# A chunked delta rule in two transformer blocks: the triangular inverses start from solved diagonal blocks of 16 instead of from the identity

## What is computed

```python
kk = heads(k * k_k)
kk = kk / jnp.maximum(jnp.sqrt(jnp.sum(kk * kk, -1, keepdims=True)), 1e-12)
k = k * (1 + (a - 1) * k_a)
decay = jnp.exp(-jnp.exp(heads(w)))
def step(S, inp):
    r_t, w_t, k_t, v_t, kk_t, b_t = inp
    sa = jnp.einsum('bhvk,bhk->bhv', S, -kk_t)
    S = S * w_t[:, :, None, :] + sa[..., None] * b_t[:, :, None, :] + v_t[..., None] * k_t[:, :, None, :]
    return S, jnp.einsum('bhvk,bhk->bhv', S, r_t)
S0 = jnp.zeros((B, H, N, N), f32)
_, y = lax.scan(step, S0, tuple(to_time(t) for t in (rh, decay, kh, vh, kk, kk * ah)))
...
bonus = jnp.sum(rh * kh * r_k, -1, keepdims=True) * vh
```

## Time and profile before

| | |
|---|---|
| median of 3 runs | 1495.6 us (1494.48 to 1495.86) |
| profiled execution | 1490.96 us |
| its span | 1489.2 us |
| mean granted clock of TensorE | 0.977 |
| DVE busy | 883.4 us, 59% |
| ACT busy | 630.5 us, 42% |
| POOL busy | 73.8 us, 5% |
| chain that ended last | PE 72%, DVE 21%, ACT 5% |
| longest group of DVE | weight remainders L1592, 374.7 us |

### The profile page before, as it was taken

The page is one execution under the profiler, slowest core; times in us unless marked ns, Lnnn a source line. Parts: engine busy times, 40 slices in busy tenths (PEclk is TensorE's granted clock), DMA queues, the critical chain, the costliest instruction groups (busy, mean ns, idle before and its releaser), DMA issues.

```text
span 1489.2 us, 21642 instructions
## 1 busy us (share of the span) xinstructions
PE 1401.2 (94%) x9280; PEld 1254.6 (84%) x9280; DVE 883.4 (59%) x1293; ACT 630.5 (42%) x899; POOL 73.8 (5%) x42
## 2 busy tenths in 40 slices
PE   7999899999899999999899999899988989799998
PEld 4676898998899997876699999898988888599997
DVE  5167534537654447554655445798988755565554
ACT  1343342534444344444543443543445544554443
POOL 0011030000200002100200000100000000000000
PEclk9999999999999999999999999998999999899999
DMA  9423000005655564622175555644544434155650
GB/s 288 147 77 113 1 1 2 1 1 198 208 188 181 189 196 129 211 85 86 57 254 172 196 172 168 198 129 161 161 133 135 148 114 163 63 198 170 196 187 29
DMA packets 154383, 204.96 MB, mean 138 GB/s; under 512 B 7440, under 2 KB 128400, under 8 KB 154160
## 3 DMA queue, kind: packets, MB, share of 16 engines
q1 hardware_dynamic: 154288, 203.59, 41.7%
HBM read 202.53 MB, written 1.05 MB: 137 GB/s over the span
## 4 chain that ended last, share of the span: by engine, by line
PE 72%; DVE 21%; ACT 5%; issue 1%; DMA 0%; SPq 0%; DVEq 0%; ACTq 0%
PE PS L465 18%; PE PS L466 17%; PE PS L467 17%; DVE PH L2049 6%; DVE WW L1592 4%; PE PS L762 3%; PE PS L749 3%; PE PS L766 2%; PE PS L665 2%; DVE AL L1631 2%; PE PS L610 1%; PE PS L715 1%; DVE PA L1855 1%; PE PS L630 1%; PE PS L646 1%
## 5 line engine op out<-in xcount | busy, mean ns | idle before, releaser
L1592 DVE TENSOR_TENSOR WW<-RG,WW 128x2048 fp32r<-128x2048 f32 x164 | 374.7, 2290 | 213.4 <-ACT WW L1118 213.2
L465 PE MATMUL PS<-AH,WW 128*128 128x256 f32 x1664 | 480.4, 289 | 16.6 <-DVE AL L1631 12.8
L466 PE MATMUL PS<-AL,WW 128*128 128x256 f32 x1664 | 475.3, 286 | 0.0
L467 PE MATMUL PS<-AH,WW 128*128 128x256 f32 x1664 | 475.1, 286 | 0.0
L1118 ACT ACTIVATE WW<-RG 128x2048 fp32r<-128x2048 f32 x164 | 311.4, 1906 | 90.7 <-PE PS L467 88.2
L465 PEld LDWEIGHTS PS<-AH,WW 128*128 128x128 f32 x1664 | 323.9, 195 | 23.7 <-issue 12.3
L466 PEld LDWEIGHTS PS<-AL,WW 128*128 128x128 f32 x1664 | 324.0, 195 | 1.6 <-issue 0.2
L467 PEld LDWEIGHTS PS<-AH,WW 128*128 128x128 f32 x1664 | 323.7, 195 | 0.0
L465 PE MATMUL PS<-WW,HH 128*128 128x512 f32 x304 | 118.8, 391 | 0.1
L466 PE MATMUL PS<-WW,HH 128*128 128x512 f32 x304 | 118.7, 390 | 0.0
L467 PE MATMUL PS<-WW,HL 128*128 128x512 f32 x304 | 118.3, 389 | 0.0
(11 more groups left out here) (270 smaller groups left out, 1771.9 us busy)
## 6 DMA issues: line engine op xcount, KB each, us to landing
RG<-in_ffn_w_in SPq DMA_DIRECT2D x44, 1024.0 KB, 5.1
RG<-in_w_ff SPq DMA_DIRECT2D x32, 1024.0 KB, 5.4
RG<-in_w_in SPq DMA_DIRECT2D x30, 1024.0 KB, 5.2
RG<-in_ffn_w_down SPq DMA_DIRECT2D x22, 1024.0 KB, 4.9
RG<-in_w_rkv SPq DMA_DIRECT2D x12, 1024.0 KB, 5.3
RG<-in_moba_w_qkv SPq DMA_DIRECT2D x12, 1024.0 KB, 5.2
RG<-in_w_o SPq DMA_DIRECT2D x4, 1024.0 KB, 9.2
RG<-in_wx_kv SPq DMA_DIRECT2D x4, 1024.0 KB, 5.9
```

The lines of the kernel that those rows point to most:

```text
L465: e.matmul(o, lh, rh, start=start, stop=False)
L466: e.matmul(o, lh, rl, start=False, stop=False)
L467: return e.matmul(o, ll, rh, start=False, stop=stop)
L1592: v.tensor_tensor(WL[lo_n % NW], ring(SPLIT[lo_n]), WH[lo_n % NW].bitcast(F32), ALU.subtract).then_inc(s_lo, 1)
```

## The change

1. **Norms on eight columns.** The sums of squares go to 8 columns (4 products against two columns). DVE bounds them with 1e-24, POOL raises them to the power -0.5, ACT spreads them to 512 columns in `qq`, and PE turns that back into the layout of the keys (`norm_spread`). Square root and reciprocal of 512 columns leave. The bonus is also taken on 8 columns and spread by the read.
2. **Two sets of buffers** for decays, k, r and kk. k always uses bank 0 and r bank 1. The key chain of step j-1 runs on DVE after the decay work of step j. All forms of half 0 are made after the key stage.
3. **Blocks of 16.** Levels 0 to 3 leave in both halves. In their place: the diagonal blocks are formed again in products of 64 by 128 by 128 (`block_form`), masked and gathered on DVE to 16 by 16 values per matrix (`block`), each row is spread by a product with a selector matrix of 0 and 1 (`block_rows`, a new ring piece `sel` of 128 by 1920 made on the host), ACT copies the rows, and DVE solves row after row (`block_inverse`), widens the result to 128 by 128 (`block_wide`), and PE turns it (`block_turn`). W uses two banks instead of four.
4. **Order.** Half 1's blocks are formed and solved inside half 0's inverse. POOL's gain and gate work is in 12 operations of 512 columns and starts after the first state. The memory turn is spread over two levels, and the group norm steps and `wo0` have new places.
5. **First pieces in two banks** (`chan_two`): the two column halves of the first piece run together over each quarter of the activation, at four places (gated FFN twice, last FFN, convolution).

Constants and norms (the first lines are SP's list):

```diff
 EARLY = ['lora', 'g1', 'v00', 'v01', 'v10', 'v11', 'k0', 'r0', 'k1', 'r1', 'k2', 'r2', 'k3', 'r3',
-         'g2', 'gn']
+         'g2', 'gn', 'sel']
...
+    put('m16', ((f >> 4) == (p >> 4)) & (p < f))
+    put('blk', (f >> 4) == (p >> 4))
+    put('eye16', (p % 16) == np.arange(16)[None, :])
...
+    return np.concatenate([((k // 16) == (m // 16)) & (k % 16 == r) for r in range(15)], 1).astype(np.float32)
...
+            piece('sel', (lambda r: r[:, 0:1920], a['sel']))
...
+            def norm_sums(j):
...
+                for q in range(4):
+                    t = e.matmul(PS[6][:, 2 * q:2 * q + 2], qq[:, q * 128:q * 128 + 128], cst('sel2'), start=True, stop=True)
+                t.then_inc(s_nm, 1)
+
+            def norm_spread(j):
+                e.wait_ge(s_nq, j + 1)
+                for q in range(4):
+                    t = e.matmul(PS[6][:, q * 128:q * 128 + 128], qq[:, q * 128:q * 128 + 128], ident, start=True, stop=True)
+                t.then_inc(s_nb, 1)
...
+                        t = e.matmul(PS[7][:, 4 * tt + 2 * m:4 * tt + 2 * m + 2],
+                                     rS2[j % 2][:, m * 256 + tt * 128:m * 256 + tt * 128 + 128], cst('sel2'), start=True, stop=True)
...
+                g.wait_ge(s_nx, j + 1)
+                own_pool.done()
+                g.tensor_tensor(RN, RN, POW, ALU.pow).then_inc(s_nr, 1)
```

PE: first pieces, blocks, the key stage and what follows it:

```diff
+            def chan_two(name, b0, b1, ready):
...
+                for k in range(8):
+                    if k % 2 == 0:
+                        e.wait_ge(s_tl, ready + k // 2 + 1)
+                    for m, b in enumerate((b0, b1)):
+                        t = mm3(e, PS[b][:, m * 256:(m + 1) * 256], wsl(name, 256, k, m * 128, m * 128 + 128), act_k(k), k == 0, k == 7)
+                t.then_inc(s_wdone, 1)
...
+            def block_form(half, pair):
+
...
+                    for t in range(2):
+                        c, h, m, pp = prob(half, pair + 2 * t, n)
+                        o_ = 256 * t + 128 * (n // 2)
+                        x = e.matmul(PS[2 + n % 2][:, o_:o_ + 128], BE[pp, m, c * 128:c * 128 + 128], AR[pp, m, c, 0, :],
+                                     start=True, stop=True)
+                    if n >= 2:
+                        x.then_inc(s_ef, 1)
...
+            def block_rows(half, b):
...
+                for r in ROWS[b]:
+                    _, lo, hi = row_at(r)
+                    t = e.matmul(PS[2 + b % 2][:, lo:hi].rearrange("p (i q) -> p i q", i=16), ring('sel')[:, 128 * r:128 * r + 128],
+                                 DB[half][:, :, r:16], start=True, stop=True)
+                t.then_inc(s_se, 1)
...
+            def block_turn(half, g, b):
...
+                for n in range(4):
+                    ns = slice(n * 128, n * 128 + 128)
+                    t = e.transpose(PS[b][:, ns], Zi[:, g, ns], ident)
+                t.then_inc(s_zt, 1)
...
+                    if j:
+                        e.wait_ge(*((s_kq, j), (s_rs_, j))[n])
                     for m in range(2):
+                        if m and n:
+                            norm_sums(j)
+                            if j == 3:
+                                block_rows(0, 2)
+                                block_rows(0, 3)
+                        elif m and j:
+                            norm_spread(j - 1)
...
+                    if n == 0 and j < 3:
+                        decay(j + 1)
+                    elif n == 0:
+                        block_rows(0, 0)
+                        block_rows(0, 1)
                 if j:
                     bonus(j - 1)
+                if j in (1, 2):
+                    block_form(0, j - 1)
+                if j == 3:
+                    block_rows(0, 4)
...
+            e.wait_ge(s_dt, 4)
+            gates(0)
...
+            e.wait_ge(s_sn, 5)
+            e.wait_ge(s_gta, 2)
+            for g in range(4):
+                block_turn(0, g, 2 + g)
+            e.wait_ge(s_gta, 4)
+            e.wait_ge(s_gk, 2)
+            e.wait_ge(s_xb, 2)
+            for g in range(4):
+                form(0, g, [0, 1, 2, 3])
...
+            e.wait_ge(s_xb, 4)
+            turned(0, [4, 5])
```

The halves on PE:

```diff
-                for l in range(7):
+                for l in range(4, 7):
                     for g in range(4):
...
+                    if half:
+                        if l < 6:
+                            memory_turn((2 * l - 8, 2 * l - 7))
+                    elif l < 6:
+                        block_form(1, l - 4)
+                    else:
+                        block_rows(1, 0)
+                        block_rows(1, 1)
+                    for g in range(4):
+                        invert_xz(half, l, g)
+                if half == 0:
+                    block_rows(1, 2)
+                    block_rows(1, 3)
+                e.wait_ge(s_wt, 12 * half + 12)
                 rhs_of(half, 0)
                 rhs_of(half, 1)
-                e.wait_ge(s_xz, 24 * half + 24)
+                if half == 0:
+                    block_rows(1, 4)
```

ACT in the halves, DVE in the key stage and the solve:

```diff
+            def rows_out(half, b):
+                n = sum(16 * (16 - r) for r in ROWS[b])
+                s.wait_ge(s_se, 5 * half + b + 1)
+                s.activation(NS[half][b], PS[2 + b % 2][:, 0:n], ACT.Copy, bias=0.0, scale=1.0).then_inc(s_sn, 1)
...
+                    for g in range(4):
+                        inverted(half, l, g)
+                    if half and l < 6:
+                        memory_turned((2 * l - 8, 2 * l - 7))
...
+                    if (half, l) == (1, 5):
+                        ahead('wo0', 0)
...
-                    if half == 1 and l == 4:
-                        ahead('wo0', 0)
...
+
...
+                v.wait_ge(s_dx, 4 * half + o + 1)
+                own_dve(v.tensor_reduce(db[:, 4 * o:4 * o + 4, :], td.rearrange("p (n b q) -> p n q b", n=4, b=8), AX, ALU.add))
...
+                    own_dve(v.tensor_copy(XC[half], eye16))
...
+            def block_inverse(half):
...
+                    for r in ROWS[b]:
+                        _, lo, hi = row_at(r)
+                        p3 = v3(PR[half][:, 0:hi - lo], 16 - r)
+                        own_dve.done()
+                        own_dve(v.tensor_tensor(p3, v3(NS[half][b][:, lo:hi], 16 - r), xc[:, :, r:16], ALU.mult))
+                        own_dve.done()
+                        own_dve(v.tensor_reduce(xc[:, :, r], p3, AX, ALU.add))
+
+            def block_wide(half, g):
...
+                for e_ in range(2):
+                    o = 8 * (g % 2) + 4 * e_ + 2 * (g // 2)
+                    z = Zi[:, g, :].rearrange("p (u e b r) -> p u e b r", u=2, e=2, b=8)[:, :, e_, :, :]
+                    xc = XC[half][:, o:o + 2, :].unsqueeze(2).broadcast_to([128, 2, 8, 16])
+                    t = v.tensor_tensor(z, xc, blk[:, 0:2, :].rearrange("p n (b r) -> p n b r", b=8), ALU.mult)
+                t.then_inc(s_zb, 1)
...
+            for j in range(4):
+                carried(j)
+                if j >= 2:
+                    block(0, 2 * j - 4)
+                    block(0, 2 * j - 3)
+                if j:
+                    keys(j - 1)
+                if j >= 2:
+                    bonus(j - 2)
+                if j < 3:
+                    decay(j + 1)
+                v.wait_ge(s_nm, j + 1)
+                own_dve.done()
+                v.tensor_scalar(RN, PS[6][:, 0:8], 1e-24, None, ALU.max).then_inc(s_nx, 1)
+            block_inverse(0)
             for g in range(4):
+                block_wide(0, g)
+            bonus(2)
+            keys(3)
+            for g in range(4):
+                formed(0, g, [0, 1, 2, 3])
                 unit(0, g)
             bonus(3)
```

The halves on DVE, and POOL:

```diff
-                for l in range(7):
...
+                    elif half == 0:
+                        block_inverse(1)
+                    elif l == 4:
+                        for step in (0, 1, 3):
+                            group_norm(1, 0, 0, step)
+                    elif l == 5:
+                        for step in (5, 6, 7):
+                            group_norm(1, 0, 0, step)
                         ahead('wo0', 0)
+                        for step in (0, 1):
+                            group_norm(2, 1, 0, step)
+                    else:
+                        for step in (3, 5, 6, 7):
+                            group_norm(2, 1, 0, step)
...
                 if half == 0:
+                    for g in range(4):
+                        block_wide(1, g)
...
-            g.wait_ge(s_xz, 8)
+            g.wait_ge(s_ss, 1)
...
+            for tt in range(2):
+                for h in range(2):
+                    sl = slice(h * 512, h * 512 + 512)
+                    own_pool(g.tensor_tensor(BV[:, tt, sl], BV[:, tt, sl], gn[:, 1024 + h * 512:1536 + h * 512], ALU.add))
+                    own_pool.done()
+                    own_pool(g.tensor_tensor(BV[:, tt, sl], BV[:, tt, sl], GT_[:, tt, sl], ALU.mult))
+                    own_pool.done()
```

(2 more changed lines are left out.)

368 lines of the change are left out of this document (219 added, 149 removed).

## The result

The changed kernel takes 1447.4 us (median of four runs, 1444.44 to 1451.19) against 1495.73 before: ratio 0.9685, 95% interval 0.9669 to 0.9702, 48 us faster. The forecast was 1443, its range 1428 to 1456. The profiled execution has a span of 1442.6 us against 1489.2, 46.6 less.

What follows compares the result with a forecast made beforehand. PE, busy 94% of the span, was taken as the bound; 34.8 - 13.3 + 24.9 + 6.0 = 52.4 us gained, giving 1438.6 in the profiled execution and 1443 at the median, range 1428 to 1456.

Steps and rivals of the forecast that it cites:

- Half 0 up to its last product: Key stage and matrix inverse of half 0: last product at 189.2 us against 224.0, 34.8 gained.
- PE sets the pace, 18.3 a step: Key stage, half 0: PE work of 18.3 us per step against 12.5 on DVE, up to step 3's norm sums.
- 1.5 for 864 columns of row products: Key stage, step 3: row products on PE priced by columns, 0.22 us per 128, 1.5 us.
- The 1.0 us for the clock: Half 0, PE going from idle to paced work at 142 to 156: 1.0 us added, between 0 and 1.9.
- The row chain: Half 0's row solve on DVE: 30 dependent small operations, 10.2 us, plus one POOL meeting of 1.2.
- small matmuls cost their weight load: Rival, key stage: small matmuls cost 0.19 us each, 5 us, first-piece gain mostly taken by remainders; 1450 us, chance 0.12.
- Rest of half 0: After half 0's last product to outputs' end: 39.4 us against 26.1, 13.3 lost, with DVE widenings priced beside POOL.
- no turn-taking on the port: Rival, half 1's widenings beside POOL: they run through at 2.7 us or in pairs; 1432 us, chance 0.20.
- Half 1: Half 1's last forms and inverse: 47.8 us against 72.7, 24.9 gained, with a hole of nearly 8 us.
- First pieces: Two-bank first pieces: 3.0 and 2.7 us at gated FFNs, 0.3 conv, 0 last FFN; 6.0 gained, between 1 and 8.
- low clock in more places: Rival: low clock over all of level 4 and after both holes, about 10 us more; 1453 us, chance 0.14.
- the power on POOL: Key stage norms on 8 columns: hidden under about 4 us; rival slower than before, over 17 us each, chance 0.03.

Runs made afterwards that it cites:

- e12: The control: the changed kernel itself, unedited, measured again beside the kernel before; 1448.9 us, ratio 0.9695.
- e11: Changed kernel with the four norm-sum products made four times in each of the four key-stage steps; 1468.2 us, ratio 0.9811.
- e1: Changed kernel with POOL's twelve gain and gate operations started after half 0's level-4 X and Z copies, not after the state; 1439.5 us, ratio 0.9644.
- e2: Changed kernel with POOL's twelve gain and gate operations waiting for the last widening of half 1 instead of the state; 1437.5 us, ratio 0.9621.
- e3: Changed kernel with ACT rounding the first output weight before half 1's level-5 copies, not after them and the memory's; 1439.8 us, ratio 0.9637.
- e7: Kernel before with only the two-bank first pieces added; 1489.3 us, ratio 0.9965.

## Why the prediction was right, point by point

**Half 0 up to its last product: 34.8 forecast, 28.7 measured.** The mechanism was right: PE paces the key stage, DVE the part from the row solve on, with the masks behind the last key chain. The 6.1 missing are 3.7 up to the start of the solve, 0.8 from there to the end of level 4, 0.5 in level 5 and 2.1 in level 6, less 1.0 for the clock.

- "PE sets the pace, 18.3 a step". It is 19.9 (76.81 to 96.71). Two-column products, taken at 0.07 between nearly nothing and 0.19, are two instructions of 0.12 each, 0.24 a product: 1.1 us a step. A block form is 1.26 and not 1.0, and four groups of projections take 14.2 and not 14.0. The solve began at 126.7 instead of 123.0.
- "1.5 for 864 columns of row products". The 18 instructions of the first two batches take 2.1 (120.06 to 122.14, and again in level 6), 0.12 each: 0.6 more at each place.
- Level 6 "8.85" took 10.9. Besides that 0.6 it holds the next two batches, 1.4 us for 800 columns, which stand ahead of the right hand sides; the forecast had them in the 2.4 us of the next piece. This is a matter of where one piece ends and the next begins.
- Level 5 took 12.3 and not 11.85, with the block form at 1.26.
- The 1.0 us for the clock was not spent in this execution: the first W product took 4.03 at 1.00. In the control it was, 5.61 at 0.79. The working set "an idle stretch of over 3 us" against paced work; the stretch ahead of 0.53 in the earlier trace rows was 2.4 us (151.5 to 153.9).
- The row chain, priced at 10.2 plus one meeting with POOL at 1.2, took 11.0 (126.66 to 137.63), with one operation of 192 elements at 0.85 instead of 0.36 beside POOL: the fixed 0.2 and 1.03 ns per element hold. The fitted figure of the Trainium skill (VectorE: DVE Perf Modes, the TRN2 errata section) gave 9.2 without the meeting, the trace has 10.5. The operations themselves follow it (0.19 for 32 elements, 0.42 for 256); the other 1.3 us are the 0.04 between one operation and the next, which my rows had and the figure has not. Its advice against tiles under 512 elements did not decide here: the faster kernel has 30 small operations in place of PE work, where PE is the bound. The eight widenings, 2.7 forecast, took 2.77.

This is the rival "small matmuls cost their weight load" in part: some 4.5 us of it (six groups of two-column products ahead of the solve, 3.3; row products, 1.2), where it was priced at 7. e11 shows the price of an instruction directly, though not that the weight load sets it.

**Rest of half 0: 13.3 lost forecast, 11.1 measured.** The state ended 8.7 us behind the last product and not 10.3, since two batches of row products had been made before. The widenings took 10.25 against 12.2 at one POOL operation each, PE's wait 7.8 against 9. The clock behind it was low (0.55 over 7 us), and the work from there to the outputs' end took 17.4 against 14.0 + 1.9. e1 and e2 show the cause, and the rival "no turn-taking on the port" (0.20) is out.

**Half 1: 24.9 forecast, 23.8 measured.** Level 5 ended 31.8 behind the outputs, forecast 30.9. PE waits 2.4 us at 242.6, where the level-4 masks stand behind the last form masks on DVE; the working named this wait ("W waits for the last masks") without a size. From the end of the level-5 products to the last product it is 17.0 (264.29 to 281.33), with 15.0 + 1.9 forecast. The hole is 7.2, and e3 shows that it was the rounding's place.

**First pieces: 6.0 forecast.** By segments 3.6, 2.7, 0.2 and 0 against 3.0, 2.7, 0.3 and 0; e7 alone 5.2. Three waits for weight remainders, 1.8 us together (at 345.3, 703.5 and 904.2), are new there, so the remainders took a part back. The end of the span shows 5.2 because the first attention lost 1.5 us (127.1 to 128.7 between common waits) at a clock of 0.97 instead of 0.99, in code that nobody touched.

**Sum.** 28.7 - 11.1 + 23.8 + 5.2 = 46.6 against 52.4. **The rivals:** low clock in more places was a part of what e12 shows, some us in some executions and not in others; the power on POOL costs 1.64 us and is hidden, as thought; the selector load took 4.6 us and nothing waited for it.

**What is not shown.** No run takes back the norms, the second set of buffers or the blocks of 16 by themselves. That the levels are what half 0 and half 1 won is read from the timeline of PE (in each half four levels of 10.72 are gone); what the norms and the buffers are worth is not measured.

## What to carry to other kernels

The change took 53 us of busy time off PE and opened two new holes of 7 to 8 us, each made by where a piece of another engine's work had been put: closing them (one line moved for each) gave two fifths as much again as the whole change. When work moves to a small chain on another engine, look at what every other engine starts at that moment, above all at GpSimd beside VectorE operations that read only SBUF, and put such work where VectorE has slack (e1). And on TensorE count instructions, not columns, for narrow products (0.12 us for one of 2 columns, the same for row products of 32 to 144, 0.11 for one of 128); a stage that PE bounds does not get faster from DVE's slack.
